# A decoder trunk on one core: where a sum of squares is taken and where a panel's low part stands in VectorE's queue

## The chip, the cores and the metric

One Trainium2 chip (trn2), of which one core is used. The metric is the device time of one execution of the program, in microseconds (us), the median of its runs. Times of single instructions come from one profiled execution, counted from the start of its span. TensorE multiplies matrices, VectorE and ScalarE do elementwise work and reductions, GpSimd only clears one tile here, and SyncE issues nearly all transfers from memory. Each engine runs its own queue in order; semaphores tie them together.

## What is computed

The reference is a two-layer decoder trunk on 256 positions of width 1024, in fp32. Each layer is a half-step SwiGLU feed-forward (FFN), a token-mixing part (attention beside a convolution module) and a second half-step FFN. Ahead of each stands the same kind of norm:

```python
def rms_norm(x, g):
    xf = x.astype(jnp.float32)
    y = xf * lax.rsqrt(jnp.mean(xf * xf, axis=-1, keepdims=True) + EPS)
    return (y * g.astype(jnp.float32)).astype(x.dtype)
...
for l in range(DEPTH):
    modulate = lambda t, i: rms_norm(t, norm_g[l, i]) * (1.0 + scale(i)) + shift(i)
    h = modulate(x, 0)
    x = x + 0.5 * gate(0) * swiglu(h, ffn_wg[l, 0], ffn_wu[l, 0], ffn_wd[l, 0])
    h = modulate(x, 1)
    ...
    x = x + gate(1) * (y @ w_out[l])
    h = modulate(x, 2)
    x = x + 0.5 * gate(2) * swiglu(h, ffn_wg[l, 1], ffn_wu[l, 1], ffn_wd[l, 1])
return rms_norm(x, final_g)
```

The change is about the passage from one such part to the next: the end of `x = x + ...`, and the norm and modulation that follow.

## The kernel before

**Tiles.** The 256 positions are two tiles of 128 rows, tile 0 and tile 1 (`tt` in the code). The residual `x` stays in SBUF. A norm of tile `tt` is: the sum of squares into `ssq` (`norm_square`, ScalarE, L721), the root of the mean into `std` (`norm_std`, ScalarE, L726), the reciprocal and the scaling of `x` into `xn_h` or `xn_q` (`norm_scale`, VectorE, L1069 and L1076), eight transposes through TensorE into PSUM (`norm_turn`, L380), and the modulation from PSUM into `hF` (`norm_full`: the first four blocks on ScalarE, L733, the other four on VectorE, L1084).

**Panels and splitting.** Weights come from memory in panels of 1 MB (128x2048) into a ring `raw` of six buffers. Most panels are multiplied in three passes: ScalarE rounds the panel to a high part `w_hi` (`hi(p)`, L708), VectorE subtracts it to get the low part `w_lo` (`lo(p)`, L997), and the activations are split in the same way into `hA_hi` (`norm_hi`, L740) and `hA_lo` (`norm_lo`, L997). TensorE then does three matmuls for one (L329, L330, L331). Some panels are used whole, in one pass (L348). The three panels that follow each of the five inner passages are all split. The program's names for them: `end` is the next part's first panel, `end + 1` and `end + 2` its second and third, `base + 3` (from the next part's side) its fourth.

**TensorE's order around a passage.** At an FFN end: the down projection of the last-but-one block for tile 1, the transposes of `mid` for tile 1, the rest of that projection, `norm_turn(n+1, 0)`, then the down projection of the last block for tile 1 (12 matmuls on `end_hi`, `end_lo`). At a mix end: `norm_turn(n+1, 0)`, then the last `w_out` for tile 1 (12 matmuls). The next part starts with `two_groups`: for tile 0, 12 matmuls each of panels `end`, `end + 1`, `end + 2`, then the transposes of tile 1, then 12 of `base + 3`; after that the same four panels for tile 1. Each panel is waited for through `ready(p)`, that is, through the low part of the panel on VectorE.

**VectorE's order** is written out by hand. At an FFN end it is `hidden(f, j, (1,))`, `mid_low(f, j, 1)` (which makes `end_lo`), `norm_scale(n + 1, 0)`, `lo(end + 1)`, `norm_full(n + 1, 0)`, two `norm_lo`, `x_update(n, 1)` (L1060 and L1065, tile 1's residual), `lo(end + 2)`. The mix end has the same tail behind `x_update(n, 0)` and `norm_scale(n + 1, 0)`.

**ScalarE's order** at an FFN end is `silu(f, j, (1,))` (L763), `norm_square(n + 1, 0)`, `preload(ACT.Sqrt)` (a table load and a one-column activation, L714), `mid_high(f, j, 1)` (which makes `end_hi`, L773), `norm_std(n + 1, 0)`, then the modulation and the high parts.

There are six passages: FFN ends f = 0, 1 and 2 (at 210, 648 and 838 us), mix ends (at 460 and 1089 us), and the last FFN end f = 3 (at 1276 us), behind which only the final norm stands. `n` counts the norms, `b` in `x_update` the residual updates.

Of the kernel before, what the change touches and what calls it, by code (L numbers as in the profile page):

```python
# [6 lines left out]
ALU = mybir.AluOpType  # L7
# [104 lines left out]
def decoder_program(nc, x_in, c_row, g_row, params, rope, ident, mask, ada_w, weights, out):  # L112
    with ExitStack() as ctx:
# [586 lines left out]
        def _(act_e):  # L700
# [85 lines left out]
            def ffn(f):  # L786
                base, n, end = ffn_base(f), ffn_norm(f), ffn_base(f) + FFN_PANELS
                if f == 0:
                    for tt in range(TT):
                        norm_full(0, tt)  # L790
                    preload(ACT.Silu)
                    hi(4)
                    for b in range(2):
                        for tt in range(TT):
                            norm_hi(0, tt, b)
                else:
                    enter(n, base, ACT.Silu)
                silu(f, 0, (0, 1))
                hi(base + 5)
                if f == 0:  # L800
                    silu(f, 1, (0, 1))
                    mid_high(f, 0)
                else:
                    mid_high(f, 0)
                    silu(f, 1, (0, 1))
                hi(base + 6)
                hi(base + 7)
                hi(base + 8)
                for j in range(2, NJ - 1):
                    pa = gate_panels(f, j)[0]  # L810
                    hi(pa + 4)
                    mid_high(f, j - 1)
                    hi(pa + 5)
                    silu(f, j, (0, 1))
                    hi(pa + 6)
                    if j == 5:
                        gate_store(n)
                    if j == 7:
                        gate_load(n)
                j = NJ - 1  # L820
                hi(end)
                mid_high(f, j - 1)
                silu(f, j, (0,))
                mid_high(f, j, 0)
                hi(end + 1)
                silu(f, j, (1,))
                norm_square(n + 1, 0)
                preload(ACT.Sqrt)
                mid_high(f, j, 1)
                norm_std(n + 1, 0)  # L830
                if n + 1 < NORMS - 1:
                    norm_full(n + 1, 0)
                    norm_hi(n + 1, 0, 0)
                    norm_hi(n + 1, 0, 1)
                    hi(end + 2)
# [159 lines left out]
        def _(dve):  # L995
# [53 lines left out]
            def x_update(b, tt):  # L1049
# [12 lines left out]
                for half in range(2):  # L1062
                    c = slice(half * 512, half * 512 + 512)
                    dve.wait_ge(xm_done, 4 * b + 2 * tt + half + 1)
                    nc.vector.tensor_tensor(x[:, tt, c], xt[:, half, :], x[:, tt, c], ALU.add).then_inc(x_done, 1)  # L1065

            def norm_recip(n, tt):
                dve.wait_ge(std_done, 2 * n + tt + 1)
                nc.vector.reciprocal(rstd[:, tt:tt + 1], std[:, tt:tt + 1]).then_inc(rstd_done, 1)  # L1069
                dve.wait_ge(rstd_done, 2 * n + tt + 1)  # L1070
# [50 lines left out]
            def ffn(f):  # L1121
                base, n, end = ffn_base(f), ffn_norm(f), ffn_base(f) + FFN_PANELS

                def ada_lo(p):
                    if f < 3:
                        ada_units(ada_before(p - 1), ada_before(p))
                    lo(p)

                if f > 0:
                    enter(n, base)  # L1130
                    hidden(f, 0, (0, 1))
                    lo(base + 5)
                    mid_low(f, 0)
                    hidden(f, 1, (0, 1))
                else:
                    lo(3)
                    lo(4)
                    hidden(f, 0, (0, 1))
                    lo(5)
                    hidden(f, 1, (0, 1))  # L1140
                    mid_low(f, 0)
                lo(base + 6)
                lo(base + 7)
                for j in range(2, NJ - 1):
                    pa = gate_panels(f, j)[0]
                    ada_lo(pa + 3)
                    mid_low(f, j - 1)
                    ada_lo(pa + 4)
                    hidden(f, j, (0, 1))
                    ada_lo(pa + 5)  # L1150
                j = NJ - 1
                lo(end - 1)
                mid_low(f, j - 1)
                hidden(f, j, (0,))
                lo(end)
                mid_low(f, j, 0)
                x_update(n, 0)
                hidden(f, j, (1,))
                mid_low(f, j, 1)
                if n + 1 == NORMS - 1:  # L1160
                    return
                norm_scale(n + 1, 0)
                lo(end + 1)
                norm_full(n + 1, 0)
                norm_lo(n + 1, 0, 0)
                norm_lo(n + 1, 0, 1)
                x_update(n, 1)
                lo(end + 2)

            def mix(l):  # L1170
# [160 lines left out]
                lo(end)  # L1331
                x_update(n, 0)
                norm_scale(n + 1, 0)
                lo(end + 1)
                norm_full(n + 1, 0)
                norm_lo(n + 1, 0, 0)
                norm_lo(n + 1, 0, 1)
                x_update(n, 1)
                lo(end + 2)

# [123 lines left out]
```

## Time and profile before

| what | value |
|---|---|
| median of three runs | 1295.67 us |
| the runs | 1293.88, 1295.67, 1295.78 us |
| span of the profiled execution | 1293.5 us |
| busy: TensorE | 1238.3 us, 96% |
| busy: VectorE | 965.1 us, 75% |
| busy: ScalarE | 547.3 us, 42% |
| chain that ended last: TensorE | 89% |
| chain that ended last: VectorE, transfers, ScalarE | 4%, 3%, 2% |
| mean granted clock of TensorE | 0.994 |

The profile gives no time of its own for the profiled execution besides its span; the median of the runs is 2.2 us above it. The granted clock is a share of 2.4 GHz. The chain that ended last is followed back from the last instruction through whatever released each step. A row of the timeline is: start and duration in us, engine, line, operation, what it writes and reads, the shapes, how many are merged, and in brackets how long the engine had been idle and what ended that. The matmuls overlap: each is shown with 0.39 us, and they start 0.23 us apart. Where a row merges several instructions, its duration is that of the whole group.

### The profile page before, as it was taken

To read this page: it belongs to the slowest core of one execution; us is meant where nothing else is said; L and a number is where in the kernel's file an instruction comes from. 1 tells how busy PE (TensorE), PEld (TensorE's weight loads), DVE (VectorE), ACT (ScalarE), POOL (GpSimd) and SP (SyncE) were. 2 spreads that over 40 slices of the span, in tenths; PEclk is the share of its full clock that TensorE was granted. 3 is DMA by queue.
4 is the path that set the end of the run, shared out by engine and by line. 5 is a ranking of instruction groups with operands and counts; after the bars stand their busy time and mean duration, and the time that the engine had idled before them with its cause. 6 is when DMAs were issued, how large, how long until landed. Compare 5 with 4: busy or idle time off the path is not lost.

```text
span 1293.5 us, 13852 instructions
## 1 busy us (share of the span) xinstructions
PE 1238.3 (96%) x5448; PEld 957.3 (74%) x5448; DVE 965.1 (75%) x1341; ACT 547.3 (42%) x576; POOL 2.2 (0%) x5
## 2 busy tenths in 40 slices
PE   3999999999998999999999999999999899999997
PEld 2588887765765787888878888876676677888885
DVE  5698886699996576988668888669999856744443
ACT  3353344532345365344354443354233454644331
POOL 0000000000000000000000000000000000000000
PEclk9999999999999999999999999999999899999999
DMA  9989994454323339889747899454432334555540
GB/s 374 417 316 378 372 377 169 163 183 159 130 98 130 137 124 376 340 340 358 294 180 280 340 343 357 174 188 174 175 130 98 130 130 169 190 190 178 204 177 33
DMA packets 52913, 293.44 MB, mean 227 GB/s; under 512 B 6640, under 2 KB 6896, under 8 KB 27120
## 3 DMA queue, kind: packets, MB, share of 16 engines
q1 hardware_dynamic: 51120, 289.38, 60.0%
q10 hardware_dynamic: 1728, 3.17, 0.7%
q8 instruction: 43, 0.70, 0.2%
q14 instruction: 22, 0.18, 0.0%
HBM read 291.45 MB, written 1.07 MB: 226 GB/s over the span
## 4 chain that ended last, share of the span: by engine, by line
PE 89%; DVE 4%; DMA 3%; ACT 2%; issue 1%; SPq 0%; DVEq 0%
PE ps L329 23%; PE ps L331 23%; PE ps L330 23%; PE ps L348 13%; DMA raw<-in_weights 2%; PE ps L537 1%; PE ps L515 1%; PE ps L396 1%; DMA ada_raw<-in_ada_w 1%; DVE w_lo L997 1%; DVE hF L1084 1%; PE ps L526 0%; PE ps L485 0%; ACT L714 0%; DVE hA_lo L997 0%
## 5 line engine op out<-in xcount | busy, mean ns | idle before, releaser
L997 DVE TENSOR_TENSOR w_lo<-raw,w_hi 128x2048 fp32r<-128x2048 f32 x176 | 401.1, 2287 | 37.6 <-ACT w_hi L708 37.3
L708 ACT CAST w_hi<-raw 128x2048 fp32r<-128x2048 f32 x176 | 334.5, 1910 | 176.8 <-DMA raw<-in_weights 113.7
L329 PE MATMUL ps<-w_hi,hA_hi 128*128 128x512 f32 (+1 forms) x992 | 395.9, 399 | 5.8 <-DVE hA_lo L997 5.8
L331 PE MATMUL ps<-w_hi,hA_lo 128*128 128x512 f32 (+1 forms) x992 | 384.3, 387 | 0.0
L330 PE MATMUL ps<-w_lo,hA_hi 128*128 128x512 f32 (+1 forms) x992 | 383.6, 387 | 0.0
L329 PEld LDWEIGHTS ps<-w_hi,hA_hi 128*128 128x128 f32 x992 | 186.9, 188 | 49.8 <-issue 15.1
L331 PEld LDWEIGHTS ps<-w_hi,hA_lo 128*128 128x128 f32 x992 | 186.7, 188 | 39.0
L330 PEld LDWEIGHTS ps<-w_lo,hA_hi 128*128 128x128 f32 x992 | 187.0, 189 | 37.9 <-issue 2.9
L1186 DVE SCALAR_TENSOR_TENSOR work<-conv_in,par,work 128x256 f32<-128x256 f32 x480 | 193.9, 483 | 0.0
L1012 DVE SCALAR_TENSOR_TENSOR product<-ada_raw,c_bc 128x1024 f32<-128x1024 f32 x144 | 171.7, 1220 | 16.0 <-DMA ada_raw<-in_ada_w 15.6
L348 PE MATMUL ps<-raw,hF 128*128 128x512 f32 x384 | 172.0, 600 | 5.5 <-ACT hF L733 5.5
L348 PEld LDWEIGHTS ps<-raw,hF 128*128 128x128 f32 x384 | 72.1, 193 | 87.0 <-issue 86.8
L329 PE MATMUL ps<-w_hi,mid_hi 128*128 128x512 f32 x336 | 131.3, 391 | 2.3 <-DVE mid_lo L997 2.3
L330 PE MATMUL ps<-w_lo,mid_hi 128*128 128x512 f32 x336 | 130.8, 389 | 0.0
L331 PE MATMUL ps<-w_hi,mid_lo 128*128 128x512 f32 x336 | 130.8, 389 | 0.0
L997 DVE TENSOR_TENSOR mid_lo<-ps,mid_hi 128x512 fp32r<-128x512 f32 (+1 forms) x44 | 29.3, 667 | 106.7 <-ACT mid_hi L770 103.3
L763 ACT ACTIVATE act<-ps 128x512 f32<-128x512 f32 (+1 forms) x48 | 27.0, 563 | 136.6 <-PE ps L331 131.7
L329 PEld LDWEIGHTS ps<-w_hi,mid_hi 128*128 128x128 f32 x336 | 63.1, 188 | 15.9 <-DVE mid_lo L997 3.0
L770 ACT CAST mid_hi<-ps 128x512 fp32r<-128x512 f32 x40 | 23.4, 586 | 120.5 <-PE ps L396 120.5
L331 PEld LDWEIGHTS ps<-w_hi,mid_lo 128*128 128x128 f32 x336 | 63.1, 188 | 13.2
L330 PEld LDWEIGHTS ps<-w_lo,mid_hi 128*128 128x128 f32 x336 | 63.1, 188 | 12.9
L1100 DVE TENSOR_TENSOR mid<-act,ps 128x512 f32<-128x512 f32 (+1 forms) x48 | 30.9, 643 | 45.1 <-ACT act L763 45.1
(121 smaller groups left out, 749.7 us busy)
## 6 DMA issues: line engine op xcount, KB each, us to landing
raw<-in_weights SPq DMA_DIRECT2D x200, 1024.0 KB, 4.9
ada_raw<-in_ada_w SPq DMA_DIRECT2D x144, 512.0 KB, 7.5
gate_bc<-gate_scratch ACTq DMA_DIRECT2D x6, 512.0 KB, 6.4
x<-in_x_tok SPq DMA_DIRECT2D x1, 1024.0 KB, 7.6
out_tok<-xn_h SPq DMA_DIRECT2D x4, 256.0 KB, 2.2
c_bc<-in_c_row SPq DMA_DIRECT2D x1, 512.0 KB, 4.6
c_bc<-in_g_row SPq DMA_DIRECT2D x1, 512.0 KB, 5.6
mask_all<-in_mask SPq DMA_DIRECT2D x1, 416.0 KB, 16.6
```

Of the source, the lines that this page charges most:

```text
L329: nc.tensor.matmul(out_ap, stat[0], mov[0], start=start, stop=False)
L330: nc.tensor.matmul(out_ap, stat[0], mov[1], start=False, stop=False)
L331: return nc.tensor.matmul(out_ap, stat[1], mov[0], start=False, stop=stop)
L348: mm = nc.tensor.matmul(out_ap, hF[:, k, t], raw[:, p % RAW, c], start=(k == 0), stop=(k == KC - 1))
L396: mm = nc.tensor.transpose(ps[:, bank, c:c + P], mid[:, tt, kk * P:(kk + 1) * P], ident_sb[:])
L708: nc.scalar.copy(w_hi[:, s % HI, :], raw[:, p % RAW, :]).then_inc(hi_done, 1)
L763: nc.scalar.activation(act[:, tts[0]:tts[-1] + 1, :], ps[:, bank + tts[0]:bank + tts[-1] + 1, 0:256], ACT.Silu).then_inc(silu_done, 1)
L770: nc.scalar.copy(mid_hi[:], cols(bank)).then_inc(mid_hi_done, 1)
L997: return nc.vector.tensor_tensor(dst, whole, hi_part.bitcast(F32), ALU.subtract)
L1012: nc.vector.scalar_tensor_tensor(out=product[:, q % 2, :], in0=ada_raw[:, q % ADA_RING, :], scalar=1.0, in1=c_bc[:], op0=ALU.mult, op1=ALU ...
L1100: nc.vector.tensor_tensor(mid[:, c, :], act[:, c, :], ps[:, bank + tts[0]:bank + tts[-1] + 1, 256:512], ALU.mult).then_inc(mid_done, 1)
L1186: nc.vector.scalar_tensor_tensor(out=work[:, c, :], in0=conv_in[:, c, t:t + T], scalar=par[:, o:o + 1], in1=work[:, c, :], op0=ALU.mult, o ...
```

## The change

`norm_square(n + 1, 0)` leaves ScalarE's queue at the FFN ends. VectorE gets a `norm_square` of its own, one `scalar_tensor_tensor` that writes `x * x` into the norm's scratch tile and the row sums into `ssq`; it stands between `hidden(f, j, (1,))` and `mid_low(f, j, 1)`. At mix ends and for tile 1 the square stays on ScalarE. And at both kinds of end `lo(end + 1)` moves from ahead of `norm_full(n + 1, 0)` to behind the second `norm_lo`.

```diff
@@ (ScalarE, ffn)
                 mid_high(f, j, 0)
                 hi(end + 1)
                 silu(f, j, (1,))
-                norm_square(n + 1, 0)
                 preload(ACT.Sqrt)
                 mid_high(f, j, 1)
                 norm_std(n + 1, 0)
@@ (VectorE)
+            def norm_square(n, tt):
+                dve.wait_ge(x_done, 4 * (n - 1) + 2 * tt + 2)
+                nc.vector.scalar_tensor_tensor(out=xn_of(n)[:, tt, :], in0=x[:, tt, :], scalar=1.0, in1=x[:, tt, :],
+                                               op0=ALU.mult, op1=ALU.mult,
+                                               accum_out=ssq[:, tt:tt + 1]).then_inc(ssq_done, 1)
@@ (VectorE, ffn)
                 hidden(f, j, (1,))
+                norm_square(n + 1, 0)
                 mid_low(f, j, 1)
                 if n + 1 == NORMS - 1:
                     return
                 norm_scale(n + 1, 0)
-                lo(end + 1)
                 norm_full(n + 1, 0)
                 norm_lo(n + 1, 0, 0)
                 norm_lo(n + 1, 0, 1)
+                lo(end + 1)
                 x_update(n, 1)
                 lo(end + 2)
@@ (VectorE, mix)
                 norm_scale(n + 1, 0)
-                lo(end + 1)
                 norm_full(n + 1, 0)
                 norm_lo(n + 1, 0, 0)
                 norm_lo(n + 1, 0, 1)
+                lo(end + 1)
                 x_update(n, 1)
                 lo(end + 2)
```

VectorE's queue at the end of f = 0, before; `mid` is the gated product of tile 1, and the two rows `w_lo<-raw,w_hi` are `lo(end + 1)` and `lo(end + 2)`:

```order
L1100 TENSOR_TENSOR mid<-act,ps 128x256
L997 TENSOR_TENSOR end_lo<-ps,end_hi 128x256
L1069 RECIPROCAL rstd<-std 128x1
L1076 TENSOR_SCALAR xn_h<-x,rstd 128x512 x2
L997 TENSOR_TENSOR w_lo<-raw,w_hi 128x2048
L1084 TENSOR_SCALAR hF<-ps,gs,modb 128x128 x4
L997 TENSOR_TENSOR hA_lo<-hF,hA_hi 128x4x128 x2
L1060 SCALAR_TENSOR_TENSOR xt<-ps,gate_bc 128x512 x2
L1065 TENSOR_TENSOR x<-xt,x 128x512 x2
L997 TENSOR_TENSOR w_lo<-raw,w_hi 128x2048
```

The same stretch after the change (its lines are numbered anew):

```order
L1105 TENSOR_TENSOR mid<-act,ps 128x256
L1068 SCALAR_TENSOR_TENSOR xn_h,ssq<-x 128x1024
L996 TENSOR_TENSOR end_lo<-ps,end_hi 128x256
L1074 RECIPROCAL rstd<-std 128x1
L1081 TENSOR_SCALAR xn_h<-x,rstd 128x512 x2
L1089 TENSOR_SCALAR hF<-ps,gs,modb 128x128 x4
L996 TENSOR_TENSOR hA_lo<-hF,hA_hi 128x4x128 x2
L996 TENSOR_TENSOR w_lo<-raw,w_hi 128x2048
L1059 SCALAR_TENSOR_TENSOR xt<-ps,gate_bc 128x512 x2
L1064 TENSOR_TENSOR x<-xt,x 128x512 x2
L996 TENSOR_TENSOR w_lo<-raw,w_hi 128x2048
```

The square has come in between `mid` and `end_lo`, and `lo(end + 1)` has moved down by six instructions, past the modulation and hA's low parts. The order of what follows is as it was. Mix ends show the same move of `lo(end + 1)` and no square.

ScalarE's queue at the end of f = 0, before:

```order
L763 ACTIVATE act<-ps 128x256
L721 ACTIVATE xn_h,ssq<-x 128x1024
L714 ACT_TABLE_LOAD
L714 ACTIVATE spare<-eps 128x1
L773 CAST end_hi<-ps 128x256
L726 ACTIVATE std<-ssq,eps 128x1
```

And after:

```order
L763 ACTIVATE act<-ps 128x256
L714 ACT_TABLE_LOAD
L714 ACTIVATE spare<-eps 128x1
L773 CAST end_hi<-ps 128x256
L726 ACTIVATE std<-ssq,eps 128x1
```

Only the square is gone. The queues of TensorE, SyncE and GpSimd are the same in both.

## Rows read from the trace of the kernel before

**Rows 1.** TensorE's waits, whole span: waiting line, releaser, us, times, longest.

```profile
PE ps L380 <- DVE xn_h L1076: 19.0, 4, 14.9
PE ps L329 <- DVE hA_lo L997: 5.8, 7, 1.4
```

**Rows 2.** Timeline of TensorE, end of f = 0: start, us, and idle before.

```profile
217.18 1.09 PE L380 MATMUL ps<-ident_sb,xn_h 128*128 128x128 f32 x8 [1.35 <-DVE xn_h L1076]
...
220.63 0.39 PE L331 MATMUL ps<-w_hi,end_lo 128*128 128x512 f32 x1
221.75 0.47 PE L329 MATMUL ps<-w_hi,hA_hi 128*128 128x512 f32 x1 [0.73 <-DVE hA_lo L997]
...
227.28 0.39 PE L329 MATMUL ps<-w_hi,hA_hi 128*128 128x512 f32 x1
```

**Rows 3.** Timeline of ScalarE, end of f = 0.

```profile
212.88 0.39 ACT L763 ACTIVATE act<-ps 128x256 f32<-128x256 f32 x1 [3.47 <-PE ps L331]
213.16 1.05 ACT L721 ACTIVATE xn_h<-x 128x1024 f32<-128x1024 f32 x1
...
214.32 1.28 ACT L714 ACT_TABLE_LOAD   x1
...
215.72 0.35 ACT L773 CAST end_hi<-ps 128x256 fp32r<-128x256 f32 x1
```

**Rows 4.** Timeline of VectorE, end of f = 0.

```profile
216.11 0.42 DVE L997 TENSOR_TENSOR end_lo<-ps,end_hi 128x256 fp32r<-128x256 f32 x1 [2.39 <-ACT end_hi L773]
...
216.64 0.88 DVE L1076 TENSOR_SCALAR xn_h<-x,rstd 128x512 f32<-128x512 f32 x2
217.44 2.29 DVE L997 TENSOR_TENSOR w_lo<-raw,w_hi 128x2048 fp32r<-128x2048 f32 x1
219.64 1.36 DVE L1084 TENSOR_SCALAR hF<-ps,gs,modb 128x128 f32<-128x128 f32 x4
220.92 1.46 DVE L997 TENSOR_TENSOR hA_lo<-hF,hA_hi 128x512 fp32r<-128x512 f32 x2
...
224.69 2.29 DVE L997 TENSOR_TENSOR w_lo<-raw,w_hi 128x2048 fp32r<-128x2048 f32 x1
```

**Rows 5.** The page's costliest groups, VectorE's modulation sums: busy us, mean ns.

```profile
L1012 DVE SCALAR_TENSOR_TENSOR product<-ada_raw,c_bc 128x1024 f32<-128x1024 f32 x144 | 171.7, 1220 | 16.0 <-DMA ada_raw<-in_ada_w 15.6
```

**Rows 6.** Timelines of TensorE and VectorE, tile 1 at the start of the first mix.

```profile
230.00 1.03 PE L380 MATMUL ps<-ident_sb,xn_h 128*128 128x128 f32 x8
...
232.89 1.29 DVE L997 TENSOR_TENSOR hA_lo<-hF,hA_hi 128x512 fp32r<-128x512 f32 x2 [0.37 <-ACT hA_hi L740]
```

**Rows 7.** Timelines of TensorE and VectorE, first mix end.

```profile
464.94 1.04 PE L380 MATMUL ps<-ident_sb,xn_q 128*128 128x128 f32 x8
...
469.11 0.47 PE L329 MATMUL ps<-w_hi,hA_hi 128*128 128x512 f32 x1 [0.38 <-DVE hA_lo L997]
...
474.66 0.39 PE L329 MATMUL ps<-w_hi,hA_hi 128*128 128x512 f32 x1
...
468.29 1.46 DVE L997 TENSOR_TENSOR hA_lo<-hF,hA_hi 128x512 fp32r<-128x512 f32 x2
...
472.06 2.28 DVE L997 TENSOR_TENSOR w_lo<-raw,w_hi 128x2048 fp32r<-128x2048 f32 x1
...
475.50 2.29 DVE L997 TENSOR_TENSOR w_lo<-raw,w_hi 128x2048 fp32r<-128x2048 f32 x1 [0.15 <-ACT w_hi L708]
```

**Rows 8.** Timeline of TensorE, last FFN end.

```profile
1282.11 0.50 PE L329 MATMUL ps<-w_hi,end_hi 128*128 128x512 f32 x1 [0.76 <-DVE end_lo L997]
```

**Rows 9.** A wait of TensorE, and stretches: busy us, then granted clock, DMA, GB/s.

```profile
443.23 0.50 PE L329 MATMUL ps<-w_hi,hB_hi 128*128 128x512 f32 x1 [2.71 <-DVE hB_lo L997]
...
440.00:445.00 5.00, 2.29 (x9) 1.59 (x8) 4.40 (x5) 0.00 (x0) 0.00 (x0) 0.93 0.92 362
445.00:450.00 5.00, 5.00 (x18) 3.90 (x18) 0.38 (x1) 0.00 (x0) 0.00 (x0) 0.73 0.00 0
217.00:222.00 5.00, 4.09 (x21) 3.29 (x22) 4.91 (x9) 3.09 (x7) 0.00 (x0) 1.00 0.54 210
```

## The prediction

> **What bounds the kernel now.** I read first the page and its chain of waits, then TensorE's list of waits, then the timelines of the places at which it waits. TensorE is 89% of the chain that ended last (the page's own share by engine, in the table above), so a microsecond counts only if TensorE waits for it. Its waits that belong to tile 0's norm are short: 19.0 us for the transposes' input in 4 waits, 14.9 of them one wait at the program's start, so 4.1 us at three FFN ends, and 5.8 us in 7 waits for low parts of the activations [rows 1]. The change acts at six places: three FFN ends with a stage behind them (f=0, 1, 2), two mix ends, and the last FFN end. The three FFN ends have the same offsets to some hundredths of a us, the two mix ends too, so one of each is worked out.
>
> **FFN end, before.** [Rows 2] are TensorE's. It stands idle 1.35 us before the transposes of tile 0 (start 217.18), the last of the 12 matmuls of tile 1's down projection starts at 220.63, and after a wait of 0.73 us for hA_lo the next stage's first panel (`end`) starts at 221.75. Panels `end` and `end+1` are 24 matmuls, and `end+2` starts at 227.28: 0.23 us a matmul, 2.72 us for the 12 of one panel and tile, plus about 0.08 us for restarting from a wait. No wait stands before `end+2`.
>
> ScalarE [rows 3] does in a row: silu (212.88 to 213.27), the square with its accumulator read (213.16 to about 214.30), the table load (214.32, 1.28), the small preload, the cast of end_hi (215.72 to 216.07). No idle time stands before the cast: what holds it is ScalarE's own queue, not the transposes that it reads.
>
> VectorE [rows 4] stands idle 2.39 us before end_lo (216.11), then goes without a gap: reciprocal, scaling of tile 0 (216.64), lo(end+1) (217.44), modulation (219.64), low parts of hA (220.92 to 222.38), x_update of tile 1, and lo(end+2), which starts at 224.69 and ends at 226.98. TensorE takes that panel at 227.28. **This is the important slack: 0.3 us.**
>
> **Step 1, the square moves to VectorE.** The nearest row for its price is the modulation sum: also scalar_tensor_tensor, 128x1024 f32, two sources in SBUF, with an accumulator, mean 1220 ns [rows 5]. It fits in the idle 2.39 us: mid ends at 213.72, the square at about 214.9. Bounds: 1.05 us (ScalarE's own square) and 2.4 us (twice the row). On ScalarE 1.04 us goes, so table load, cast and std come 1.04 us earlier; the cast then ends at 215.03, still behind the square, so the square on VectorE costs nothing. If it ran over 1.4 us, it would take the cast's place as the last arrival. So scaling starts at 215.60 and the transposes at 217.18 - 1.04 = 216.14; 0.3 us of the 1.35 stay.
>
> The Trainium skill (Vector Engine (DVE) Microarchitecture Reference, section 7, "Points that are easy to get wrong") says that this form with two non-bf16 SBUF sources runs at half throughput, since no read port is left for the accumulator. The trace speaks against a penalty on top of the 1220 ns.
>
> **Step 2, lo(end+1) moves behind tile 0's norm.** What it removes from ahead of the modulation is 2.20 us (217.44 to 219.64). But modulation can't start then, since it waits for the transposes. Tile 1 at the next stage's start shows the chain without anything in its way [rows 6]: transposes at 230.00, hA's low parts from 232.89 to 234.18, so 2.89 and 4.18 us after the transposes' start. With 0.05 us for the restart and the transposes at 216.14, the low parts run from 219.1 to 220.37; the first is done at 219.8. TensorE, with its down projection shifted by 1.04, is free at 220.86 - 1.04 = 219.8, so the 0.73 us wait goes too, and panel `end` starts at about 219.9 instead of 221.75. That is a lead of 1.8 us.
>
> **What is late next.** VectorE now stands idle where lo(end+1) was its filler: from the scaling's end (216.48) until the transposes are done (about 217.3), and again 0.4 us until ScalarE's cast of hA_hi. All its work stays to be done. Behind the low parts come lo(end+1), 2.20 us, done at about 222.6, for which TensorE comes at 222.7 (no wait, but nothing to spare), then x_update and lo(end+2). From the end of hA's low parts to the end of lo(end+2) it was 226.98 - 222.38 = 4.60 us; now it is 2.20 more, so lo(end+2) ends at 220.37 + 2.20 + 4.60 = 227.17, 0.2 us later than before. TensorE is ready for `end+2` at 219.9 + 0.08 + 5.44 = 225.4 and waits about 1.7 us. With 0.06 to 0.14 us from VectorE's end to TensorE's start and 0.08 for the restart it stands at 227.35 against 227.28 before. **The lead of 1.8 us is given back whole; an FFN end changes by +0.07 us** (+0.03 to +0.11), three by +0.2.
>
> **Mix end.** There the square stays on ScalarE, tile 0's transposes start at 464.94 with no wait, and only step 2 acts [rows 7]. Before, hA's low parts run from 468.29 to 469.75 (TensorE's panel `end` at 469.11, a wait of 0.38 us), lo(end+2) ends at 472.06 + 2.28 = 474.34, and TensorE takes `end+2` at 474.66. After: the low parts end at 464.94 + 4.17 = 469.11, lo(end+1) at 471.3, lo(end+2) at 469.11 + 2.20 + 4.59 = 475.90. TensorE gets its 0.4 us at `end`, then waits about 1.7 us for `end+2` and takes it up at 475.98, 0.08 more for the restart: 476.08 against 474.66, **+1.42 us** (1.35 to 1.5), two of them +2.84. VectorE had no idle here before; it gets 1.2 us ahead of the modulation and 0.4 ahead of the low parts, and that is the loss. The square of tile 1 waits for x_update, and the cast of panel `end+3` stands behind it on ScalarE; lo(end+3) waits for that cast, ends at 475.50 + 2.29 = 477.79 before, and moves by the 1.55 us of x_update, to 479.34. TensorE comes for it at 476.08 + 2.72 and some 0.8 for tile 1's transposes, 479.6, so nothing grows further.
>
> **Last FFN end.** No stage follows, so step 1 alone acts: TensorE waits 0.76 us for end_lo and starts at 1282.11 [rows 8]. With end_lo 1.04 us earlier it starts when free: 0.9 us, plus 0.1 of restart, **-1.0 us**, which goes straight to the end (bounds -0.8 and -1.04).
>
> **Sum:** 0.2 + 2.84 - 1.0 = +2.1 us (1.5 to 2.6). Queues of SP and POOL get nothing moved. The profiled span is 1293.5 us; the span becomes 1295.6. The median of the runs, 1295.67, lies 2.2 above the span, and the runs themselves differ by 1.9. So **1297.8 us**, +0.16%, within the 0.2% (2.6 us) that a measurement of this kernel can tell from no change.
>
> **Rivals.** *Slower by the clock.* After the wait of 2.71 us at 443.23 the granted clock is 0.93 and then 0.73 over two stretches of 5 us, that is, the lower level of 1.2 GHz for a part of them: (0.07 + 0.27) x 5 = 1.7 us lost [rows 9]. The change makes five waits of some 1.7 us. For it: waits of this kind do that. Against: around the FFN end, with waits of 1.35 and 0.73 us, the clock stayed 1.00 [rows 9]. It decides once two of the five waits end so: +3.4, 1301.2 us. Fewer such stretches than before at places that have them already would give 1.7 back, at random.
>
> *The square is slower than its row.* At 2.4 us it would end at 216.1, as end_lo did before; step 1 then gains nothing, the transposes stay at 217.18, lo(end+2) comes 1.0 later still. Three times 1.1, plus 2.84: +6.1, 1301.8 us. The row at 1220 ns speaks against it. By the rule of the Trainium skill (Vector Engine (DVE) Microarchitecture Reference, section 7), taken as a doubling of the row, the time would be this one.
>
> *Faster: `end+2` isn't late.* If lo(end+2) were done before TensorE comes (225.4), the leads would stay: three of 1.8, two of 0.45, and 1.0 at the end: -7.3, 1288.4 us. It needs 1.7 us of VectorE work to be hidden; against it speaks that VectorE's queue is in order and full from the low parts on.
>
> *Absorbed.* Later waits of TensorE for other chains could take up part of the mix ends' delay: +0.5, 1296.2 us. What releases them is itself released by TensorE's progress, through panel_done, so I give it little.
>
> **How the numbers follow.** Forecast 0.70, clock 0.12, slow square 0.04, faster 0.05, absorbed 0.09. The forecast lies only 0.5 us under the bound of +2.6, and the runs scatter by 1.9, so a third of its 0.70 falls above. Slower: 0.23 + 0.12 + 0.04 = 0.39; same: 0.47 + 0.08 = 0.55; faster 0.06. Range 1295.6 to 1301.2: 2 us under the forecast for scatter and absorption, up to the clock rival above.
>
> **What would show it.** Right: transposes of tile 0 at FFN ends 1.0 us earlier with some 0.3 us of wait; no wait for hA_lo; five new waits of TensorE for w_lo, some 1.7 us each, 5.44 us after panel `end`; VectorE idle 0.8 to 1.2 us between scaling and modulation; no wait for end_lo at the last end. Wrong: no wait for w_lo, a square well over 1.4 us, or end_lo released by VectorE's own queue; at the mix ends, an `end+2` that isn't later. The sum is wrong, too, if the five waits are followed by a granted clock under 1.

## The result, and the profile after

| | before | after |
|---|---|---|
| median of runs (lowest to highest), us | 1295.72 (1293.88 to 1296.83) | 1300.82 (1296.97 to 1301.12) |
| ratio to before, 95% interval | | 1.0031 (1.0020 to 1.0042) |
| span of the profiled execution, us | 1293.5 | 1298.9 |
| mean granted clock | 0.994 | 0.992 |

The change makes the kernel slower by about 0.3%. The forecast was 1297.8 us, +0.16%, with a range of 1295.6 to 1301.2. The time lies in the range, near its upper end, and beyond the 0.2% within which I had put the larger chance.

The page of after, busy time by engine, shows hardly any new work: what the change does to the time is in the waits.

```profile
PE 1241.6 (96%) x5440; PEld 958.2 (74%) x5448; DVE 970.5 (75%) x1349; ACT 542.1 (42%) x568; POOL 2.2 (0%) x5
```

TensorE's waits of after, whole span (waiting line, releaser, us, times, longest), against [rows 1]:

```profile
PE ps L380 <- DVE xn_h L1081: 16.0, 4, 15.0
PE ps L329 <- DVE w_lo L996: 7.9, 5, 1.6
PE ps L329 <- DVE hA_lo L996: 2.9, 2, 1.4
```

The wait for the transposes' input fell from 19.0 to 16.0 us, that for hA_lo from 5.8 to 2.9, in 2 places where there were 7. (These two, 1.44 us at 424.36 and 1.42 us at 1053.60, stand inside the two mixes and at no passage; before has them too.) In their stead stand five waits for w_lo, 7.9 us, which before had none. The timeline of TensorE in after at the end of f = 0, against [rows 2], has all three:

```profile
217.16 1.09 PE L380 MATMUL ps<-ident_sb,xn_h 128*128 128x128 f32 x8 [0.32 <-DVE xn_h L1081]
...
220.63 0.39 PE L331 MATMUL ps<-w_hi,end_lo 128*128 128x512 f32 x1
220.94 0.47 PE L329 MATMUL ps<-w_hi,hA_hi 128*128 128x512 f32 x1
...
228.26 0.50 PE L329 MATMUL ps<-w_hi,hA_hi 128*128 128x512 f32 x1 [1.56 <-DVE w_lo L996]
```

The absolute times of both kernels almost agree here only because this execution of after came to the place 1.0 us late. The first transposes wait 0.32 us instead of 1.35, panel `end` starts with no wait right behind the down projection (220.94), and `end+2` then waits 1.56 us. VectorE in after over the same stretch, against [rows 4]:

```profile
214.65 1.22 DVE L1068 SCALAR_TENSOR_TENSOR xn_h<-x 128x1024 f32<-128x1024 f32 x1
215.79 0.09 DVE L1068 DVE_READ_ACCUMULATOR xn_h<-x 128x1 f32 x1
216.09 0.42 DVE L996 TENSOR_TENSOR end_lo<-ps,end_hi 128x256 fp32r<-128x256 f32 x1 [0.21 <-ACT end_hi L773]
...
216.62 0.88 DVE L1081 TENSOR_SCALAR xn_h<-x,rstd 128x512 f32<-128x512 f32 x2
218.37 1.36 DVE L1089 TENSOR_SCALAR hF<-ps,gs,modb 128x128 f32<-128x128 f32 x4 [0.86 <-PE ps L380]
220.10 1.29 DVE L996 TENSOR_TENSOR hA_lo<-hF,hA_hi 128x512 fp32r<-128x512 f32 x2 [0.37 <-ACT hA_hi L740]
221.32 2.28 DVE L996 TENSOR_TENSOR w_lo<-raw,w_hi 128x2048 fp32r<-128x2048 f32 x1
...
225.92 2.28 DVE L996 TENSOR_TENSOR w_lo<-raw,w_hi 128x2048 fp32r<-128x2048 f32 x1
```

The square takes 1.22 us and fits in idle time: end_lo still waits 0.21 us for ScalarE's cast. Then come two pieces of idle time that [rows 4] don't have, 0.86 and 0.37 us, and lo(end+2) ends at 228.20, where TensorE picks it up at 228.26. At the first mix end, TensorE and VectorE in after, against [rows 7]:

```profile
467.40 1.04 PE L380 MATMUL ps<-ident_sb,xn_q 128*128 128x128 f32 x8
...
471.12 0.47 PE L329 MATMUL ps<-w_hi,hA_hi 128*128 128x512 f32 x1
...
478.44 0.50 PE L329 MATMUL ps<-w_hi,hA_hi 128*128 128x512 f32 x1 [1.59 <-DVE w_lo L996]
...
468.55 1.37 DVE L1089 TENSOR_SCALAR hF<-ps,gs,modb 128x128 f32<-128x128 f32 x4 [1.19 <-PE ps L380]
...
476.10 2.29 DVE L996 TENSOR_TENSOR w_lo<-raw,w_hi 128x2048 fp32r<-128x2048 f32 x1
```

From tile 0's transposes to `end+2` it is 11.04 us here (467.40 to 478.44) and was 9.72 (464.94 to 474.66), so +1.32. The 12 matmuls from there to tile 1's transposes take 2.86 us instead of 2.72, which is +0.14 for restarting from the wait.

**How the places are measured from here on.** Absolute times are of little use, since each execution drifts by 1 or 2 us on its way. I take a *passage*: from the start of tile 0's x_update on VectorE to the start of tile 1's transposes on TensorE. It begins ahead of everything that the change touches and ends behind `end+2`, and at the three FFN ends of one kernel it agrees to 0.04 us. In brackets stands its first part, to the start of tile 0's transposes. The last FFN end, which has no tile-1 transposes behind it, is measured from the start of tile 0's x_update on VectorE to the end of the span.

| us | three FFN ends | mix end 1 | mix end 2 | last end |
|---|---|---|---|---|
| before | 19.77, 19.80, 19.80 (6.95) | 17.61 (5.17) | 17.60 (5.16) | 17.74 |
| after | 19.89, 19.88, 19.87 (5.91) | 19.06 (5.16) | 18.73 (4.82) | 17.11 |

In the mean of the three FFN ends the first part fell by 1.03 us and the rest rose by 1.12. At mix ends the whole loss is in the second part: 13.90 and 13.91 us instead of 12.44. (At mix end 2 the passage starts 0.35 us late; that is not a gain, see e7 and e9.) In sum: 3 x 0.09 + 1.46 + 1.47 - 0.63 = **+2.6 us**, the last term being the last end (17.11 against 17.74).

The two profiled spans differ by more, 5.4 us. Of that 3.2 is in the passages (with the late start of the last of them) and the last end gives back 0.6; 1.0 had been lost before the first of them (TensorE's first wait for mid_lo ends at 56.67 instead of 55.64), 0.2 lies in another wait for mid_lo, and 1.6 us is one more stretch in which the clock was at its lower level: while TensorE works there are four in this execution of after and three in that of before, at other places. The windows of one of them show it, first after, then before (busy us, then granted clock, DMA share, GB/s):

```profile
380.00:385.00 5.00, 3.65 (x24) 2.99 (x22) 4.01 (x11) 4.74 (x5) 0.00 (x0) 0.98 0.37 121
385.00:390.00 5.00, 5.00 (x15) 3.12 (x15) 3.85 (x5) 1.44 (x1) 0.00 (x0) 0.68 0.21 88
```

```profile
380.00:385.00 5.00, 3.55 (x27) 2.97 (x26) 3.31 (x9) 4.97 (x5) 0.00 (x0) 1.00 0.59 210
385.00:390.00 5.00, 5.00 (x19) 2.67 (x18) 4.61 (x8) 0.95 (x2) 0.00 (x0) 1.00 0.00 0
```

That stretch stands in the mix, behind a wait of 1.35 us for probsT which before has too (1.45 us there, and no fall of the clock), and not behind one of the new waits. Whether these 2.8 us belong to the change was the first question for the experiments.

### The profile page after: what moved, and what is told of

It reads as the page before. It is cut to its first block, busy times and chain, and to the rows that moved or that the text cites. A ratio compares the mean times of both kernels' runs of the same rounds, so it can differ in the third digit from the quotient of the medians.

```text
span 1298.9 us, 13844 instructions
## 1 busy us (share of the span) xinstructions
PE 1241.6 (96%) x5440; PEld 958.2 (74%) x5448; DVE 970.5 (75%) x1349; ACT 542.1 (42%) x568; POOL 2.2 (0%) x5
## 3 DMA queue, kind: packets, MB, share of 16 engines
HBM read 291.45 MB, written 1.07 MB: 225 GB/s over the span
## 4 chain that ended last, share of the span: by engine, by line
PE 88%; DVE 6%; DMA 3%; ACT 2%; issue 1%; SPq 0%; DVEq 0%; ACTq 0%
PE ps L329 23%; PE ps L331 22%; PE ps L330 22%; PE ps L348 13%; DVE w_lo L996 2%; DMA raw<-in_weights 2%; PE ps L537 1%; PE ps L515 1%; PE ps L396 1%; DMA ada_raw<-in_ada_w 1%; ACT hF L733 1%; DVE hA_lo L996 1%; PE ps L380 1%; DVE xt L1059 1%; DVE x L1064 1%
## 5 line engine op out<-in xcount | busy, mean ns | idle before, releaser
L1011 DVE SCALAR_TENSOR_TENSOR product<-ada_raw,c_bc 128x1024 f32<-128x1024 f32 x144 | 171.7, 1220 | 15.5 <-DMA ada_raw<-in_ada_w 15.1
L348 PE MATMUL ps<-raw,hF 128*128 128x512 f32 x384 | 174.8, 608 | 5.5 <-ACT hF L733 5.5
```

What stands on the lines that cost most here:

```text
L348: mm = nc.tensor.matmul(out_ap, hF[:, k, t], raw[:, p % RAW, c], start=(k == 0), stop=(k == KC - 1))
L1011: nc.vector.scalar_tensor_tensor(out=product[:, q % 2, :], in0=ada_raw[:, q % ADA_RING, :], scalar=1.0, in1=c_bc[:], op0=ALU.mult, op1=ALU ...
```

## The experiments

### The change again, beside its parts

Run a2 is the change itself, unedited, once more. e1 is the square alone: the change with lo(end+1) put back at both kinds of end. e2 is the reordering alone: before, with both lo(end+1) moved. e3 is the change with the mix ends put back.

```diff
(e1: this at FFN ends and at mix ends; e3: at mix ends only)
                 norm_scale(n + 1, 0)
+                lo(end + 1)
                 norm_full(n + 1, 0)
                 norm_lo(n + 1, 0, 0)
                 norm_lo(n + 1, 0, 1)
-                lo(end + 1)
                 x_update(n, 1)
```

```diff
(e2, against before: at FFN ends and at mix ends)
                 norm_scale(n + 1, 0)
-                lo(end + 1)
                 norm_full(n + 1, 0)
                 norm_lo(n + 1, 0, 0)
                 norm_lo(n + 1, 0, 1)
+                lo(end + 1)
                 x_update(n, 1)
```

> The change itself once more, beside the kernels below. Read by its passages it is 2.1 us slower than before (FFN ends +0.05 each, mix ends +1.42 each, last end -1.07), yet its first median stood 5 us above. If the rest is chance (the start, and where the granted clock falls), the difference shrinks to some 2 to 4 us with more runs (ratio 1.0016 to 1.003). If something lasting stands outside the six passages, it stays at 5 us (1.004), and shows in the trace at the same place as before.

> Only the square moves to VectorE; lo(end+1) stays ahead of the modulation. Theory (VectorE's queue up to lo(end+2) is the bound): all of tile 0's norm and lo(end+2) come 1.04 us earlier at three FFN ends, the waits for hA_lo (0.7) stay, no wait for w_lo appears, and the last end gives 1.0: -4.1 us, ratio 0.9968. Rival (the clock, or an accumulating square that costs more than it frees): no gain or a loss, 1.000 or above.

> Only lo(end+1) moves; the square stays on ScalarE. Theory: each FFN end loses 1.15 us (VectorE's idle time ahead of the modulation and of the low parts), each mix end 1.42, the last end nothing: +6.3 us, ratio 1.0049, with five waits for w_lo of some 1.6 us. Rival (the loss is the clock's): the passages themselves show less, and the loss sits in stretches of granted clock under 1.

> The change with the old order at the two mix ends. Theory: mix ends as before, three FFN ends +0.05 each, the last end -1.0: -0.85 us, ratio 0.9993, so 2.9 us faster than the change. Rival (mix ends are not where it is lost): as slow as the change.

| | ratio (95%) | median | FFN ends | mix ends | last end |
|---|---|---|---|---|---|
| a2 | 1.0020 (1.0012 to 1.0029) | 1298.83 | 19.88, 19.87, 19.91 | 19.06, 18.73 | 17.21 |
| e1 square alone | 0.9976 (0.9966 to 0.9986) | 1292.81 | 18.75, 18.75, 18.75 | 17.61, 17.60 | 17.09 |
| e2 reordering alone | 1.0037 (1.0025 to 1.0049) | 1300.65 | 20.91, 20.91, 20.90 | 19.06, 19.06 | 17.78 |
| e3 mix ends put back | 1.0002 (0.9993 to 1.0011) | 1296.28 | 19.91, 19.88, 19.87 | 17.59, 17.63 | 17.01 |

**a2** has every passage of after to 0.04 us and a span 4.9 us shorter, with a mean clock of 0.996 instead of 0.992. So the 2.8 us of start and clock belong to that one execution, and the +2.6 of the passages is what the change costs; a2's ratio is just that (1.0020, 2.6 us), and the two intervals overlap between 1.0020 and 1.0029. How little one span tells at this size a2 shows from the other side, too: its 1294.0 is only 0.5 above before's, since it has one stretch of low clock fewer than that execution of before (two against three). Nor do the runs as a whole say much more: a2's twelve lie between 1295.77 and 1301.23 us, the 26 of before that were run beside them between 1293.83 and 1297.03. Whether the wider scatter belongs to the change, the runs don't show.

**e1** is the square alone, and it gains at each FFN end the 1.04 us that step 1 expects. In all it gains less than the 4.1 us expected, 3.4 us by its places: the last end gives 0.65 us and not 1.0, and the second mix end loses 0.33 us (both are taken up below). Its ratio, 0.9976, is 3.1 us. TensorE in e1 at the end of f = 0:

```profile
216.25 1.09 PE L380 MATMUL ps<-ident_sb,xn_h 128*128 128x128 f32 x8 [0.32 <-DVE xn_h L1081]
...
220.81 0.47 PE L329 MATMUL ps<-w_hi,hA_hi 128*128 128x512 f32 x1 [0.70 <-DVE hA_lo L996]
...
229.08 1.04 PE L380 MATMUL ps<-ident_sb,xn_h 128*128 128x128 f32 x8
```

The first wait is short, as in after; the wait for hA_lo stays, 0.70 us (0.73 before); and there is no wait for w_lo. Panel `end` comes 4.56 us behind the transposes, as in [rows 2] (4.57), and all that follows keeps the gain. In e1 VectorE has no gap in front of the modulation (w_lo 216.50 for 2.28, modulation 218.70): lo(end+1) lies where VectorE would wait for the transposes.

**e2** is the reordering alone: each FFN end loses 1.11 us and each mix end 1.46. TensorE in e2 at the end of f = 0:

```profile
217.24 1.09 PE L380 MATMUL ps<-ident_sb,xn_h 128*128 128x128 f32 x8 [1.36 <-DVE xn_h L1076]
...
228.34 0.50 PE L329 MATMUL ps<-w_hi,hA_hi 128*128 128x512 f32 x1 [1.57 <-DVE w_lo L997]
...
231.19 1.03 PE L380 MATMUL ps<-ident_sb,xn_h 128*128 128x128 f32 x8
```

The gain of the square and the loss by the order add up: -1.04 + 1.11 = +0.07 a passage, against +0.09 in after. The loss has the size of the idle time that lo(end+1) left behind: VectorE has gaps of 0.86 and 0.37 us in e2 at the FFN ends, 1.23 together, and 1.19 and 0.37 in after at the first mix end, 1.56 together. By so much lo(end+2) comes later against the transposes (1.25 and 1.58 us), and TensorE had 0.3 us to spare. By the passages e2 should be +6.3 us, its ratio gives 4.8 (3.2 to 6.4). e3 says the same from the other side: with the mix ends put back, what is left of the change by its places is 0.3 at the FFN ends, 0.35 at the second mix end, which starts late here too, and -0.73 at the last end, close to nothing. It measures 1.0002, where 0.9993 was expected. This settles where the +2.6 is: at the two mix ends.

### What makes `end+2` late: the length of VectorE's queue

My account says that lo(end+2) is late because everything behind the low parts is full, so that any work taken out of there should come back as time. A rival would be that lo(end+2) waits for its own input (ScalarE's w_hi, or the DMA). e4 takes work out of tile 1's x_update between lo(end+1) and lo(end+2): it leaves out three quarters of the columns, so tile 1's residual is wrong in it, and it serves for its times alone. The same edit cuts the slices of `acc` and `xt`.

```diff
             def x_update(b, tt):
+                w = 128 if tt == 1 and b < GROUPS - 1 else 512
...
-                    c = slice(half * 512, half * 512 + 512)
+                    c = slice(half * 512, half * 512 + w)
```

> The change, with tile 1's residual update at the five inner passages cut to 128 of 512 columns in each of its four instructions (three quarters of that update are left out). It takes some 1.6 us of VectorE work from ahead of lo(end+2) and nothing else. Theory (the wait for w_lo is VectorE's queue): the wait of 1.6 us at each of the five passages falls to about 0.1, each passage is 1.6 us shorter, 8 us less than the change, ratio to before about 0.996. Rival (the wait follows the transposes or ScalarE, not the amount of VectorE work): as slow as the change, 1.0023.

Measured: 0.9953 (0.9938 to 0.9968), median 1289.13. The passages are 18.27 at all three FFN ends and 17.46 and 17.13 at mix ends: 1.60 to 1.62 us shorter than after, each. The timelines of VectorE and TensorE in e4 at the end of f = 0:

```profile
222.14 0.48 DVE L1060 SCALAR_TENSOR_TENSOR xt<-ps,gate_bc 128x128 f32<-128x128 f32 x2
...
222.94 2.28 DVE L996 TENSOR_TENSOR w_lo<-raw,w_hi 128x2048 fp32r<-128x2048 f32 x1
...
225.28 0.50 PE L329 MATMUL ps<-w_hi,hA_hi 128*128 128x512 f32 x1
...
228.13 1.03 PE L380 MATMUL ps<-ident_sb,xn_h 128*128 128x128 f32 x8
```

The wait in front of `end+2` is gone: the matmul before it starts at 224.90, lo(end+2) ends at 225.22, and TensorE starts at 225.28, 0.15 us behind its own pace. Nothing was done to `end+2`'s input, and the passage fell by as much as VectorE had less to do. So the wait was for the length of that queue, and the rival is out.

e5 keeps all the work and only puts lo(end+2) ahead of x_update of tile 1. The late panel should come in time, and the question is what is late next.

```diff
                 lo(end + 1)
-                x_update(n, 1)
                 lo(end + 2)
+                x_update(n, 1)
```

> The change, with lo(end+2) moved ahead of tile 1's residual update at all five passages. Theory (the same VectorE work is only put off): no wait for w_lo at end+2, but tile 1's square, the scaling and above all the low part of panel end+3 come 2 us later, and TensorE waits there some 2.5 us: each passage 1.9 us longer than in the change, ratio to before about 1.0097. Rival (the order at end+2 was the whole loss): the gain of 1.8 us at an FFN end and 0.4 at a mix end is kept, ratio 0.996.

Measured: 1.0155 (1.0132 to 1.0177), median 1316.28: slower by 20 us, where about 12.5 was expected. TensorE's waits for w_lo in e5, whole span, and its timeline and windows at the first mix end:

```profile
PE ps L329 <- DVE w_lo L996: 11.5, 5, 2.3
...
481.94 1.09 PE L380 MATMUL ps<-ident_sb,xn_q 128*128 128x128 f32 x8 [1.10 <-DVE xn_q L1081]
485.34 0.60 PE L329 MATMUL ps<-w_hi,hA_hi 128*128 128x512 f32 x1 [2.30 <-DVE w_lo L996]
...
481.00:486.00 5.00, 1.76 (x10) 1.42 (x11) 4.06 (x7) 3.98 (x7) 0.00 (x0) 0.96 0.00 0
486.00:491.00 5.00, 5.00 (x17) 3.97 (x17) 2.30 (x5) 3.90 (x4) 0.00 (x0) 0.70 0.00 0
```

The wait at `end+2` is gone, and two stand in its place: 1.10 us at tile 1's transposes, since its square, std and scaling all follow x_update, and 2.30 us at `end+3`. That is the expected shift. What was not expected is the clock: at each of the five places it falls behind these two waits (0.63 in the 5 us from 870). So the mechanism of the prediction's *slower by the clock* is real, but the new waits of 1.6 us didn't set it off. The windows at the new wait in after, first mix end:

```profile
475.00:480.00 5.00, 3.41 (x16) 2.50 (x15) 4.82 (x7) 3.24 (x4) 0.00 (x0) 1.00 0.07 30
480.00:485.00 5.00, 5.00 (x27) 3.97 (x26) 4.00 (x7) 2.96 (x7) 0.00 (x0) 1.00 0.00 0
```

The clock stays at its upper level. It is so at all five places in both after and a2. The length of a wait alone doesn't decide it: the stretch at 385 us in after came behind one of 1.35 us.

### Can the square's gain be kept, and the low part be moved to use?

If an instruction in front of the modulation costs nothing because VectorE would wait there anyway, then other idle time should do as well. In [rows 4] VectorE waits 2.39 us in front of end_lo, of which the square uses half; and ahead of tile 0's update at FFN ends it waits longer still. e8 is e1 with lo(end+1) at FFN ends moved into that idle time; e10 does the same at mix ends, ahead of tile 0's scaling, too.

```diff
(e8, against e1, FFN ends)
                 lo(end)
                 mid_low(f, j, 0)
+                lo(end + 1)
                 x_update(n, 0)
...
                 norm_scale(n + 1, 0)
-                lo(end + 1)
                 norm_full(n + 1, 0)
```

```diff
(e10, against e8, mix ends)
                 x_update(n, 0)
-                norm_scale(n + 1, 0)
                 lo(end + 1)
+                norm_scale(n + 1, 0)
                 norm_full(n + 1, 0)
```

> The square on VectorE, the old order at mix ends, and at FFN ends lo(end+1) put ahead of tile 0's residual update, where VectorE stands idle for 4.7 us. Theory: the cast that it needs ends only 0.8 us before that update, so the update comes 1.4 us later and the transposes of mid 0.5; tile 0's transposes come 0.55 later than with the square alone, but hA_lo and lo(end+2) are then in time: each of three FFN ends 1.27 us shorter than before, ratio 0.9970. Rival: the late update costs more than the gap gives, and it is slower than the square alone (0.9976).

> The last kernel with lo(end+1) in VectorE's idle time at the FFN ends, and at mix ends too, between tile 0's residual update and the reciprocal, where VectorE is idle for 1.5 us. Theory: the scaling comes 0.65 us later, the transposes 0.25, but the low part is out of the way of the modulation: panel end and end+2 0.2 us earlier than before at each mix end, 0.4 us in all, ratio to before 0.9967. Rival: the later scaling costs what the move gives, 0.9970 or above.

Measured: e8 0.9970 (0.9958 to 0.9981), median 1291.26; e10 0.9960 (0.9946 to 0.9973), median 1290.78. The timeline of VectorE in e8 at the end of f = 0 shows the place that was found:

```profile
209.22 2.29 DVE L996 TENSOR_TENSOR w_lo<-raw,w_hi 128x2048 fp32r<-128x2048 f32 x1 [3.94 <-ACT w_hi L708]
211.43 1.28 DVE L1059 SCALAR_TENSOR_TENSOR xt<-ps,gate_bc 128x512 f32<-128x512 f32 x2
```

Here the update itself begins later, so the passage (17.13) can't be compared; from ScalarE's cast of `end+1` to tile 1's transposes it is 21.28 us against 22.50 before, 1.22 less, where e1 has 1.04. At mix ends e10 has 17.42 twice against 17.61, as VectorE and TensorE show at the first of them:

```profile
462.17 2.28 DVE L996 TENSOR_TENSOR w_lo<-raw,w_hi 128x2048 fp32r<-128x2048 f32 x1
...
468.89 0.47 PE L329 MATMUL ps<-w_hi,hA_hi 128*128 128x512 f32 x1
```

There lo(end+1) runs while VectorE would wait for std, and panel `end` starts without its wait of 0.38. Both kernels beat before and after. Which of e1, e8 and e10 is fastest the intervals don't tell; by the sums of their places (-3.4, -3.9 and -4.3 us, with the late start at the second mix end counted in each) it is e10.

### The last end, and the late instruction

Two sizes in the table of passages were not in the prediction. First, the last end gave 0.63 us where 1.0 had been worked out. In after, VectorE's last update starts 1.07 us earlier behind tile 0's update (8.36 us instead of 9.43), so the step itself did as expected; but from there to the end of the span it is 8.75 us instead of 8.31. The page's list of DMA issues has the stores of the output (KB each, median us to landing) at

```profile
out_tok<-xn_h SPq DMA_DIRECT2D x4, 256.0 KB, 2.6
```

where before it was 2.2. e6 tells whether that goes with the square: it is e1, with the last end's square back on ScalarE.

```diff
(e6, against e1; VectorE)
                 hidden(f, j, (1,))
-                norm_square(n + 1, 0)
+                if f < 3:
+                    norm_square(n + 1, 0)
(ScalarE)
                 silu(f, j, (1,))
+                if f == 3:
+                    norm_square(n + 1, 0)
                 preload(ACT.Sqrt)
```

> As the kernel with the square alone, but at the last FFN end the square is back on ScalarE. Theory: the last end loses what it gained, the wait of 0.76 us for end_lo returns, the stores of the output land in 2.2 us again: 0.7 us slower than the square alone (0.9976), ratio to before about 0.9981. Rival (the slower stores have nothing to do with the square): they stay at 2.6 us, and the ratio is 0.9985.

Measured: 0.9979 (0.9970 to 0.9988), median 1293.20; FFN ends 18.77, 18.77, 18.74, last end 17.7 as before, and stores of 2.2 us. Over all traces: 2.5 to 2.8 us in after, a2, e1, e3, e4, e5, e8 and e10, where the last square is on VectorE; 2.2 in before, e2, e6, e7 and e9, where it isn't. So the slower stores go with the last square's place, and from the last update to the end of the span e1 takes 8.73 us and e6 8.30, 0.43 less: that much of the 1.07 they take. Why, the runs don't show.

Second, at the second mix end in after, tile 0's update starts 0.35 us late. VectorE stands idle 1.64 us before it instead of 1.30, though the releaser is the same. e1 has it, e2 hasn't. Is it the square, or just the number of instructions ahead of it in VectorE's queue? The square adds six by then (two at each of three FFN ends). e7 adds two tiny memsets at each FFN end in before, at the square's place, and e9 four.

```diff
(e7, against before; e9 has four such lines; `idle` is a tile of their own)
                 hidden(f, j, (1,))
+                nc.vector.memset(idle[:, 2 * f:2 * f + 1], 1.0)
+                nc.vector.memset(idle[:, 2 * f + 1:2 * f + 2], 1.0)
                 mid_low(f, j, 1)
```

> The kernel before, with two one-column memsets on VectorE in its idle time at each FFN end. In every kernel so far with the square on VectorE the second mix end's residual update starts 0.35 us later against TensorE's matmuls (4.8 us ahead of the transposes, not 5.16), and the stores of the output take 2.6 us, not 2.2. If that is the position of instructions in VectorE's queue, it shows here too; if it is the square itself, all is as before.

> The kernel before with four one-column memsets at each FFN end instead of two. Two made the second mix end's residual update start 0.35 us late, as the square does. If that is a place in VectorE's queue at which one instruction comes late, 12 more instructions ahead of it instead of 6 put it on another one: the second mix end goes back to 5.16 us from the update to the transposes, or the delay shows elsewhere. If any added instruction does it, it stays at 4.81.

Tile 0's update at the second mix end, VectorE's timeline, in e7 and in e9:

```profile
1089.66 1.29 DVE L1061 SCALAR_TENSOR_TENSOR xt<-ps,gate_bc 128x512 f32<-128x512 f32 x2 [1.63 <-PE ps L332]
```

```profile
1089.12 1.29 DVE L1061 SCALAR_TENSOR_TENSOR xt<-ps,gate_bc 128x512 f32<-128x512 f32 x2 [1.28 <-PE ps L332]
```

Each of the two was run once (1296.38 and 1296.10 us), so only their traces count. With six more instructions (e7) it is late, the wait for hA_lo behind it is 0.71 us instead of 0.38; with twelve (e9) it is on time, with a wait of 0.38. So it is a matter of position in the queue, and not of the square. It costs nothing in the change, where the wait for w_lo swallows it (from tile 0's transposes to tile 1's it is 13.90 and 13.91 us at the two mix ends), and 0.33 us in e1. What the engine does at that position no view shows, and the cause is open. The stores were 2.2 us in both e7 and e9.

## Why the prediction was right, and where it was off

**Step 1, the square.** Right in mechanism and size. It was priced at 1.22 us from the modulation sums [rows 5] and took 1.22, plus 0.08 for reading the accumulator, which the price left out and which its cover hid. Transposes came 1.04 us earlier with 0.32 us of wait left (0.3 predicted), and end_lo was released by ScalarE's cast.

**The rival of a slow square** (by the Trainium skill, Vector Engine (DVE) Microarchitecture Reference, section 7, taken as a doubling of the row) is ruled out by that 1.22 us: two fp32 sources in SBUF with an accumulator, 1024 elements, no slower than the row. The doubling was a wrong reading of the rule from the start, since the row in [rows 5] is of that same form and would have had any such loss in its 1220 ns. Nor does the trace show a loss against two fp32 sources without an accumulator: tile 1's `x<-xt,x` takes 1.28 us for two of 128x512.

**Step 2 and what is late next.** Right. Panel `end` had no wait, lo(end+2) became the last arrival by the order of VectorE's queue, and the whole lead of 1.8 us went. Predicted +0.07 for an FFN end, measured +0.09; predicted +1.42 for a mix end, measured +1.46 and +1.47. Waits of "some 1.7 us" were 1.56 to 1.59; the last matmul of `end+1` starts at 226.30, so `end+2` could have started 0.23 later, 5.59 us behind `end` (5.44 + 0.08 predicted). Counted from there it waits 1.73 us; the profile's 1.56 counts from the end that it gives the last matmul. The gap ahead of the modulation was 0.86 us at FFN ends, 1.19 at the first mix end and 0.87 at the second, whose update was late (0.8 to 1.2 predicted). One reading was wrong and did no harm: of the seven waits for hA_lo in [rows 1] only five, 3.0 us, belong to tile 0's norm, and the other two stand inside the mixes. e4 shows that the queue's length is the cause and e2 that the order alone makes it.

**The last end** is the term that was mis-sized: -1.0 predicted, -0.63 measured, outside its bounds of -0.8 and -1.04. The step from row to price was right as far as end_lo and the last update; it went wrong at "which goes straight to the end", since the stores behind it took 0.43 us longer. This is 0.37 of the 0.5 us between +2.1 and +2.6; the rest is under 0.1 us at the FFN ends together and 0.1 at the mix ends.

**The numbers.** +2.1 was taken to be within 0.2% with more chance than beyond it. The sum by places is +2.6, just at the bound, and the two measurements say 1.0031 and 1.0020. The sum is near by its mechanism; that the first median, 5.1 us above before, still lay in the range is in part luck, since the upper end, 1301.2, was set by the clock rival, which didn't happen. The step that failed is the one from a sum 0.5 us under the bound to a chance of 0.55 for "same": I had set the bounds of the sum at 1.5 to 2.6, and left no room at all above them for a term that I did not see. The first profiled span, 5.4 us longer, would have made a story of its own; half of it was one execution's start and clock.

**The clock rival.** Not what happened: none of the ten new waits in after and a2 was followed by a lower clock (nor any of e2's five), so its condition, two of five, was never met. The time it gave, 1301.2, is close to the first median, 1300.82, and that is a coincidence, as a2 shows. e5 shows that the mechanism exists, with waits of 1.1 and 2.3 us close together.

**The "faster" rival** fell with the five waits: `end+2` is late. But e1, e8 and e10 show where the gain that it hoped for can be had: keep the square on VectorE, and leave lo(end+1) where VectorE must wait anyway. **"Absorbed"** fell as well: no other wait takes up the passages' losses. Between one passage and the next, after and a2 differ from before only by stretches of lower clock, by the late update of the second mix end, and by some 0.2 us in other waits.

## What to carry to other kernels

In an in-order queue an instruction that stands where its engine must wait for another one costs little or nothing there. Moved behind that point it leaves its old place idle, and all that follows comes later by that idle time: here 1.23 us at an FFN end and 1.56 at a mix end, for an instruction of 2.2. So before moving one out of a consumer's way, follow the queue on to the next thing that somebody waits for; here its slack was 0.3 us against 2.2 us moved. And measure such changes from a fixed event ahead of the place to a fixed event behind it: that gave 0.04 us of scatter where whole executions of one kernel lay 3 to 5 us apart.

## What the runs showed of the hardware

- A VectorE instruction can start 0.35 us late for no reason found but its position in the queue: with six instructions more ahead of it, be they squares or one-column memsets, and not with none or twelve (e7, e9). It was seen at one place of the program, in ten traces; e9, with twelve, is a single trace.
- The stores of the output took 2.5 to 2.8 us to land instead of 2.2 wherever the last sum of squares ran on VectorE, 8 traces against 5. The cause is open.
- TensorE's clock stayed at its upper level behind the ten single waits of 1.56 to 1.59 us for w_lo, fell behind one of 1.35 us for probsT (after, 0.68 in the 5 us from 385) and not behind one of 1.45 at the same place of before, fell behind 2.71 us in some executions and not in others (0.93 and 0.73 in [rows 9]; in after 1.00 behind the one that ends at 447.31, and 0.77 in the 5 us from 1075 behind the one that ends at 1076.54), and fell behind all five pairs of 1.1 and 2.3 us in e5, some 7 us more there than the waits were expected to cost.
